# Building a gate table on one Trainium2 core: two slots of eight tokens in place of four slots of four

## The reference

```python
q = (xt @ w_q).reshape(T, PEER_HEADS, 2, PEER_DHALF)
s = jnp.einsum('thcd,hcnd->thcn', q, sub_keys)
s1v, s1i = lax.top_k(s[:, :, 0], PEER_TOPK)          # 16 of 128 first halves
s2v, s2i = lax.top_k(s[:, :, 1], PEER_TOPK)          # 16 of 128 second halves
...
top_s, top_pos = lax.top_k(cand, PEER_TOPK)          # 16 of the 256 pairs
eidx = jnp.take_along_axis(cidx, top_pos, axis=-1)   # expert = first * 128 + second
gates = jax.nn.softmax(top_s, axis=-1)
...
a = jnp.einsum('td,ted->te', xs, u[es])
hact = jax.nn.gelu(a) * gs
return jnp.einsum('te,ted->td', hact, v[es])
```

## Time and profile before

| | us |
|---|---|
| median of 3 runs | 3561.41 (3547.05, 3561.41, 3562.57) |
| the profiled execution | 3550.87 |
| its span, first to last instruction | 3549.1 |
| matmuls of the gate table, first start to last start (L1678) | 1282.1 to 1415.0 |
| last copy of the table starts (L1734) | 1417.2 |

### The profile page before, as it was taken

One profiled execution on the slowest core, in us unless ns is written; L12 is line 12 of the kernel. 1 busy time (PEld: TensorE's weight loads), 2 busy tenths in 40 slices (PEclk: granted clock), 3 DMA queues, 4 the chain that ended last, 5 costly groups with the idle time before them and its releaser, 6 DMA issues.

```text
span 3549.1 us, 51460 instructions
## 1 busy us (share of the span) xinstructions
PE 3359.0 (95%) x16926; PEld 2944.6 (83%) x16926; DVE 2226.8 (63%) x3877; ACT 1116.9 (31%) x1732; POOL 1165.7 (33%) x870
## 2 busy tenths in 40 slices
PE   7999999878989947999999999999999999999999
PEld 5778876667877746898998998998998998999998
DVE  2003412795028898677777777777777777777776
ACT  3122223443232259322233233222332232222322
POOL 2344431264435410322322323323333333323332
PEclk9999999899999979999999999999999999999999
DMA  4223320002332124888887887888888887888876
GB/s 140 73 87 95 95 83 21 25 1 101 95 107 81 56 94 184 316 265 265 268 267 259 274 265 262 270 265 263 271 264 265 269 267 262 271 267 263 269 262 234
DMA packets 276021, 686.85 MB, mean 194 GB/s; under 512 B 120544, under 2 KB 120800, under 8 KB 273504
## 3 DMA queue, kind: packets, MB, share of 16 engines
q1 hardware_dynamic: 202224, 417.51, 36.3%
q0 software_dynamic: 73728, 268.47, 22.5%
HBM read 655.48 MB, written 30.41 MB: 193 GB/s over the span
## 4 chain that ended last, share of the span: by engine, by line
PE 59%; ACT 2%; issue 1%; DMA 1%; ACTq 0%; DVE 0%; DVEq 0%; SPq 0%
PE exp_a L1900 10%; PE exp_a L1902 10%; PE exp_a L1901 10%; PE exp_o L1921 10%; PE exp_o L1923 10%; PE exp_o L1919 10%; ACT table_gaps L1718 1%; ACT table_stage L1734 1%; DMA gate_table<-table_stage 0%; PE table_b L1678 0%; ACTq L1718 0%; DMA exp_raw<-in_v 0%; ACTq L1734 0%; DVE table_hot L1704 0%; PE table_t L1669 0%
## 5 line engine op out<-in xcount | busy, mean ns | idle before, releaser
L1900 PE MATMUL exp_a<-x_high,exp_uh 128*128 128x384 f32 x2048 | 686.4, 335 | 10.6 <-DVE exp_ul L1984 10.6
L1902 PE MATMUL exp_a<-x_high,exp_ul 128*128 128x384 f32 x2048 | 686.0, 335 | 0.0
L1901 PE MATMUL exp_a<-x_low,exp_uh 128*128 128x384 f32 x2048 | 686.0, 335 | 0.0
L1923 PE MATMUL exp_o<-exp_vh,exp_al 128*128 128x512 f32 x1536 | 598.2, 389 | 0.0
L1921 PE MATMUL exp_o<-exp_vl,exp_ah 128*128 128x512 f32 x1536 | 598.1, 389 | 0.0
L1919 PE MATMUL exp_o<-exp_vh,exp_ah 128*128 128x512 f32 x1536 | 597.5, 389 | 0.0
L1879 POOL DMA_INDIRECT exp_rows<-in_v_rows,exp_now x256 | 329.0, 1285 | 707.9 <-DVE h L2005 656.4
L1879 POOL DMA_INDIRECT exp_rows<-in_u_rows,exp_now x256 | 299.5, 1170 | 733.5 <-DVE exp_rows L1998 688.5
L1949 ACT CAST exp_vh<-exp_raw 128x1024 fp32r<-128x1024 f32 x256 | 260.1, 1051 | 516.4 <-PE exp_o L1923 493.1
L1984 DVE TENSOR_TENSOR exp_vl<-exp_raw,exp_vh 128x1024 fp32r<-128x1024 f32 x256 | 304.5, 1220 | 165.7 <-ACT exp_vh L1949 165.7
L1900 PEld LDWEIGHTS exp_a<-x_high,exp_uh 128*128 128x128 f32 x2048 | 385.8, 188 | 12.3 <-DVE exp_ul L1984 7.3
(11 more groups left out here) (290 smaller groups left out, 5180.6 us busy)
## 6 DMA issues: line engine op xcount, KB each, us to landing
exp_raw<-in_u SPq DMA_DIRECT2D x256, 512.0 KB, 5.2
exp_raw<-in_v SPq DMA_DIRECT2D x256, 512.0 KB, 4.4
w_in_raw<-in_w_in SPq DMA_DIRECT2D x88, 512.0 KB, 3.6
gate_table<-table_stage SPq DMA_DIRECT2D x6, 4096.0 KB, 11.6
exp_gates<-gate_table SPq DMA_DIRECT2D x128, 192.0 KB, 5.3
w_out_raw<-in_w_out SPq DMA_DIRECT2D x32, 512.0 KB, 3.6
w_q_raw<-in_w_q SPq DMA_DIRECT2D x32, 512.0 KB, 3.9
x_rows<-in_x SPq DMA_DIRECT2D x4, 1024.0 KB, 7.9
```

What stands on the lines that cost most here:

```text
L1900: pe.matmul(bank, uh[:, b, c, :], xh[:, 0:DENSE_TB, c, :], start=(c == 0), stop=False)
L1901: pe.matmul(bank, uh[:, b, c, :], xl[:, 0:DENSE_TB, c, :], start=False, stop=False)
L1902: last = pe.matmul(bank, ul[:, b, c, :], xh[:, 0:DENSE_TB, c, :], start=False, stop=(c == DC - 1))
L1923: last = pe.matmul(bank[:, :], al[:, key, tokens], vh[:, dc % 2, key, :], start=False, stop=(key == KEYS_OF_MACRO - 1))
```

## The change

The number of slots goes from four to two and the tokens of a slot from four to eight. A pass of the loops stays at 16 tokens and the `hot` tiles keep their total size. PSUM tiles for the table: before four of one bank each, after two of two banks each. The tile for gaps, `table_gaps`, had two halves for the two odd slots; there is one odd slot now, so one piece of twice the size. The last edit only writes a count in terms of `SLOTS`.

```diff
-SLOTS, SLOT_TOKENS = 4, 4
+SLOTS, SLOT_TOKENS = 2, 8
...
-        gaps = place("table_gaps", [P, 2, SLOT_TOKENS, NK], F32, 88)
+        gaps = place("table_gaps", [P, SLOTS // 2, SLOT_TOKENS, NK], F32, 88)
...
-                            match(s, i * run + rounds * run, i * 2 + (2 * rounds + s // 2 + 1))
+                            match(s, i * run + rounds * run, i * (SLOTS // 2) + (SLOTS // 2 * rounds + s // 2 + 1))
```

## The result

| | before | after |
|---|---|---|
| median of 4 runs | 3559.70 us (3547.05 to 3562.57) | 3591.03 us (3586.79 to 3604.54) |
| the profiled execution | 3550.87 us | 3593.59 us |
| its span | 3549.1 us | 3591.8 us |

The ratio is 1.0112, with a 95% interval from 1.0085 to 1.0139: the change makes the kernel slower by about 1.1% (the two medians alone stand 0.9% apart, inside the interval), and the forecast was 3589 us, +0.95%.

What follows compares the result with a forecast made beforehand. ScalarE was taken to bound the kernel before, its closed loop with TensorE after. Loop with start +27.9 us and clock +6 gave +34 us; from the middle 3555.5, forecast 3589 us, +0.95%, range 3573 to 3602 (chance 0.68), outer 3568 to 3618.

Steps and rivals of the forecast that it cites:

- The circle: Closed loop of ScalarE's Relu, slot 1's matmuls, their copy and next squares: 6.70 us a pass against 5.58, +26.9 us.
- ScalarE's own work: ScalarE's copies, squares and Relu per pass fall from 5.58 to 5.23 us; alone this would give 8.4 us back.
- VectorE at 5.6 us under cover: VectorE's slot 0 work plus TensorE's matmuls take 5.6 us a pass, hidden by ScalarE's 6.70 us loop; adds nothing.
- Start and end: Gate-table stage's edges: first matmul 1.6 us later, start makes +27.9 of +26.9; end adds nothing.
- The cover of the end: After the last copy, the 1.6 us later casts and matmuls are hidden by the 13.63 us store and following load.
- The clock: TensorE's idle gaps halve its clock in about five of 24 passes, up to 1.3 us each: +6 us.
- The rule of the Trainium skill: Matmul engine scales power with utilization, so matmuls belong back to back; alone it puts the sum toward the upper bound.
- ScalarE as the bound: Rival: ScalarE finds slot 1's matmuls done, pass 5.23 us, -8.4 us, 3547 us; chance 0.05.
- A looser circle: Rival: cheaper large instructions and hand-back, pass near 6.1 us, +8 to +15 us, 3567 us; chance 0.11.
- a costlier PSUM tile: Rival: copies over two banks may pay each start, 0.46 us more a pass, +11, 3600 us; no separate chance, inside range.
- the clock in most passes: Rival: TensorE's clock falls in most passes of the stage, +59 us, 3614 us; chance 0.13.
- The other rule: Grouping into larger operations can improve throughput where the engine is saturated; by it the time would be 3547 us.

Runs made afterwards that it cites:

- both_ahead: match_ahead with slot 0's ones' side also given a second tile, made by VectorE ahead of its wait, and Relu in place; stage 137.0 us, ratio to kernel before 0.9991.
- match_ahead: Changed kernel plus a second tile for the odd slot's ones' side, so ScalarE does match before copying slot 1; stage 143.9 us, ratio to kernel before 1.0007.
- the fillers: Changed kernel plus 16 matmul instructions of the identity into a spare bank behind slot 0 in each pass; stage 169.5 us, ratio to kernel before 1.0086.
- no_ones_on_vector: Changed kernel with VectorE's L1699 done once ahead of the loop, not in the 24 passes (wrong table for slot 0); stage 180.3 us, one execution 3600.02 us.
- relu_in_halves: Changed kernel with L1722 (Relu) as two instructions of 512 elements, TensorE awaiting the second only before the fifth token; stage 170.2 us, ratio to kernel before 1.0086.
- two_slots_of_four: Kernel before with two slots in place of four, still four tokens each; stage 186.6 us, ratio to kernel before 1.0104.
- pool_distances: Kernel before (four slots of four) with GpSimd subtracting for the ones' sides of slots 1 to 3, ScalarE doing the rest; stage 177.0 us, ratio 1.0124.

## Why the prediction was right

- **The circle.** Worked out at 6.70 us, measured 6.67. Its parts: `Relu` 1.06 (1.05), to TensorE 0.05 (0.05), matmuls and back 2.18 (2.05 + 0.16), copy to `Square` 0.91 (0.90), squares 2.47 (2.49). ScalarE stands 1.33 by the timeline; the forecast of 1.47 counted from the point where it could have begun. That the circle costs the time is shown from three sides: opened, it gives back 36 us, the 12.2 of the clock among them; with small groups it costs as much and more; and with `Relu` in halves its parts, 0.78 + 2.14 + 0.91 + 2.47, again add up to the pass of 6.30.
- **ScalarE's own work** at 5.23 us a pass is shown by both_ahead at 5.24. The gain of 0.35 is real and was hidden by the circle.
- **VectorE** at 5.6 us under cover: match_ahead, which takes the cover off, runs at 5.54.
- **Start and end.** The first matmul starts 7.2 us behind the first transpose (1282.0 to 1289.23), where it was 5.6: 1.6 later, as forecast. The first two slots then took 5.89 us, not 6.67, so the first copy of slot 1 came 13.2 us behind the first transpose and not 14.2. The cover of the end held: what lies behind the last copy takes 2130.0 us against 2131.3.
- **The clock** is the term that was mis-sized. The step was "about five passes in 24, +6 us", at up to 1.3 us each; it was ten passes and 12.2 us, up to 1.73 each, so the rest of the stage's 38.5 us is 26.3 against a forecast of 27.9. The price of 1.3 was too low because 6.67 / 2 = 3.3 counts only the distances from start to start, while the 2.05 it was set against holds the last instruction's length too: at half clock the 16 took 3.79. By the fillers, which keep the clock whole, the stage is 10.4 us shorter; their first pass, still at half clock, is longer by 1.8 (its two copies lie 3.89 us apart where they lay 2.09), so all later passes together gain the 12.2. The rule of the Trainium skill that the prediction cited, in "Perfetto Trace Analysis", Matmul Optimizations, agrees in its direction; by it alone the sum was to lie toward the upper bound of 31 us, and 12.2 were measured.
- **The rivals.** ScalarE as the bound needs the circle open and is both_ahead's case. A looser circle and a costlier PSUM tile are excluded by the 6.67 and 5.24 us; the clock in most passes did not come about; it fell in ten of 24. The other rule cited from that page of the Trainium skill, in Optimizing Scalar/DVE Operations, that grouping helps a saturated engine, holds only once the circle is open: there the stage is 4.4 us shorter than before, here 38.5 longer.
- **The time.** Medians gave +31 us, the ratio +40, the stage +38.5, against +34. That the median after, 3591.03, lies 2 us from the forecast is in part luck: the stage lost 4.5 us more than forecast, and the part ahead of the stage, which scatters by up to 16 us, is in both numbers.

What stays open: which part of the 5.6 us ahead of the stage is chance, and how the stage itself scatters, as each kernel has one profile. The closest thing to a second one, no_ones_on_vector, gave the stage 0.4 us longer.

## What to carry to other kernels

Count for each buffer in turn how far the engine that fills it may run ahead of the engine that empties it. With one odd slot, ScalarE's next input to TensorE stood behind its own wait for TensorE's last output, and the pass became the sum of both engines' work for a slot in place of the larger. Larger groups lower the fixed costs and lengthen that sum; they pay only when the look-ahead is kept, which here took a second tile of 4 KB a partition for alternate passes, and an order of work in which nothing that the other engine needs is queued behind a wait for it.

## What was not expected of the hardware

- TensorE lost its clock in 10 passes of 24 with gaps of up to 2.8 us between 4 us of work, in 7 of 24 with gaps of 2.50 us (relu_in_halves), and in none with gaps of 1.70 us (two_slots_of_four) or 1.28 us (match_ahead). With such gaps filled by matmuls that nobody needs, the stage is 10.4 us shorter.
- GpSimd's `TENSOR_TENSOR` slowed VectorE's `TENSOR_SCALAR` of 128x128 badly: median 335 ns, but up to 1207 with GpSimd at work. Of the 384, 75 took over 400 ns, and each of these lay beside a GpSimd subtraction; the 247 that lay beside none took at most 341. VectorE's `TENSOR_TENSOR` of 128x512 stayed at 674 to 693; beside nine of them GpSimd's own instruction took 1.10 to 1.63 us, where the other 66 took 1.03 to 1.20. Two forms of one tile in pool_distances (shortest, median, longest in ns):

```profile
L1703 DVE TENSOR_SCALAR table_hot<-c_iota,picksT x384: 328/335/1207, 1292.0 to 1461.6; 128x128 f32<-128x128 f32 x192
...
L1698 DVE TENSOR_TENSOR table_hot<-c_iota,picksT x24: 674/679/693, 1291.4 to 1454.8; 128x512 f32<-128x512 f32 x24
```
